# Delta rule: the first head's stages from the turning of the inverse on, two positions later

## The reference, cut to what matters

```python
a_mat = where(strict, einsum('bhnid,bhnjd->bhnij', k_beta, k) * decay, 0.0)
t_inv = triangular_solve(a_mat + eye, eye, lower=True, unit_diagonal=True)
u = einsum('bhnij,bhnjd->bhnid', t_inv, v * beta)
w = einsum('bhnij,bhnjd->bhnid', t_inv, k_beta * exp(g))
...
v_new = u_n - w_n @ state                 # step over the chunks
out   = q_n @ state + intra_n @ v_new
state = state * d_n + k_n.T @ v_new
```

## Time and profile before

| | |
|---|---|
| time, median of 3 runs | 1989.81 us (1989.42 to 1990.35) |
| the profiled execution's own time | 1988.39 us |
| its span, first to last instruction | 1986.6 us |
| PE busy | 1957.0 us (99%), 12159 instructions |
| DVE busy | 1385.5 us (70%) |
| ACT busy | 978.1 us (49%) |
| POOL busy | 518.5 us (26%) |
| mean granted TensorE clock | 0.998 |

### The profile page before, as it was taken

One profiled execution on the slowest core, in us unless ns is written; L12 is line 12 of the kernel. 1 busy time (PEld: TensorE's weight loads), 2 busy tenths in 40 slices (PEclk: granted clock), 3 DMA queues, 4 the chain that ended last, 5 costly groups with the idle time before them and its releaser, 6 DMA issues.

```text
span 1986.6 us, 30677 instructions
## 1 busy us (share of the span) xinstructions
PE 1957.0 (99%) x12159; PEld 1730.5 (87%) x12159; DVE 1385.5 (70%) x1928; ACT 978.1 (49%) x1472; POOL 518.5 (26%) x530
## 2 busy tenths in 40 slices
PE   9999999999999999999999999999999999999998
PEld 7898998787788998998898999878888888989996
DVE  6964977588747955973894696376776558946963
ACT  5543653445645633653562464355564555524642
POOL 1201311454221301311130221157566011301311
PEclk9999999999999999999999999999999999999999
DMA  5232332444122232332233223223222122332331
GB/s 190 99 124 86 107 131 72 124 134 130 54 85 96 107 119 84 110 127 82 94 116 109 85 107 127 77 71 97 75 71 93 55 95 96 115 109 85 117 128 43
DMA packets 63168, 199.97 MB, mean 101 GB/s; under 512 B 12816, under 2 KB 14896, under 8 KB 63024
## 3 DMA queue, kind: packets, MB, share of 16 engines
q1 hardware_dynamic: 59616, 196.55, 29.1%
q10 hardware_dynamic: 3408, 1.44, 0.3%
HBM read 188.51 MB, written 2.38 MB: 96 GB/s over the span
## 4 chain that ended last, share of the span: by engine, by line
PE 87%; DVE 6%; ACT 3%; issue 2%; POOL 1%; DMA 1%; SPq 0%; ACTq 0%; DVEq 0%; POOLq 0%
PE prod L592 16%; PE prod L594 15%; PE prod L593 15%; PE misc L686 6%; PE misc L688 6%; PE misc L687 6%; PE prod L686 4%; PE prod L688 4%; PE prod L687 4%; PE misc L907 2%; DVE h_lo L1621 1%; ACT L1445 0%; ACT h_hi L1158 0%; PE misc L786 0%; PE prod L752 0%
## 5 line engine op out<-in xcount | busy, mean ns | idle before, releaser
L592 PE MATMUL prod<-h_hi,p_hi 128*128 128x512 f32 x728 | 300.3, 413 | 2.2 <-DVE p_lo L1505 1.3
L594 PE MATMUL prod<-h_hi,p_lo 128*128 128x512 f32 x728 | 284.9, 391 | 0.0
L593 PE MATMUL prod<-h_lo,p_hi 128*128 128x512 f32 x728 | 284.0, 390 | 0.0
L592 PE MATMUL prod<-a_hi,d_hi 128*128 128x512 f32 x693 | 270.0, 390 | 0.0
L593 PE MATMUL prod<-a_lo,d_hi 128*128 128x512 f32 x693 | 270.0, 390 | 0.0
L594 PE MATMUL prod<-a_hi,d_lo 128*128 128x512 f32 x693 | 269.9, 389 | 0.0
L2102 POOL TENSOR_TENSOR s_f<-raw 128x512 f32<-128x512 f32 x70 | 94.4, 1348 | 670.0 <-DVE s_lo L1580 360.0
L1505 DVE TENSOR_TENSOR d_lo<-raw,d_hi 128x1408 fp32r<-128x1408 f32 x64 | 104.0, 1626 | 232.5 <-ACT d_hi L1072 232.5
L1072 ACT ACTIVATE d_hi<-raw 128x1408 fp32r<-128x1408 f32 x64 | 88.3, 1380 | 219.4 <-PE prod L594 218.9
L1505 DVE TENSOR_TENSOR p_lo<-raw,p_hi 128x1024 fp32r<-128x1024 f32 x86 | 111.9, 1301 | 75.5 <-ACT p_hi L1072 75.3
L592 PEld LDWEIGHTS prod<-h_hi,p_hi 128*128 128x128 f32 x728 | 137.1, 188 | 30.8 <-issue 8.5
(11 more groups left out here) (371 smaller groups left out, 5266.4 us busy)
## 6 DMA issues: line engine op xcount, KB each, us to landing
raw<-in_w SPq DMA_DIRECT2D x252, 512.0 KB, 3.5
raw<-in_wd SPq DMA_DIRECT2D x64, 704.0 KB, 4.1
blk<-blocks SPq DMA_DIRECT2D x16, 256.0 KB
x<-in_x SPq DMA_DIRECT2D x8, 256.0 KB, 5.7
k_dup<-k_dup SPq DMA_DIRECT2D x8, 256.0 KB, 3.5
silu_g<-g_rows SPq DMA_DIRECT2D x7, 256.0 KB, 4.6
out<-y_out SPq DMA_DIRECT2D x12, 128.0 KB, 2.0
raw<-in_w SPq DMA_DIRECT2D x4, 256.0 KB, 5.5
```

The source lines that it names most:

```text
L592: pe.matmul(bank, wh, hi, start=k == 0, stop=False)
L593: pe.matmul(bank, wh, lo, start=False, stop=False)
L594: ins = pe.matmul(bank, wl, hi, start=False, stop=k == tiles_n - 1)
```

## The change

In the first head alone, the seven stages `turn`, `y5`, `t5`, `y6`, `t6`, `y7` and `t7` get positions of their own. Until now they followed from `CHAIN1`: 36 plus 12, 14, 16, 18, 20, 22 and 24, so 48, 50, 52, 54, 56, 58 and 60. They come to stand at 50, 52, 54, 56, 58, 60 and 61. The first six are moved by two positions, the last by one. `new0` stays at 62. All four engines take their part of a stage from this table, so the parts on PE, ACT and DVE are moved alike; POOL and SP have no part in these seven stages.

```diff
 SLOT_0 = {"spread": 10, "decay": 14, "mask": 15, "tri": 16, "kk": 14, "amat": 17, "blocks": 18, "lvl5": 19, "qdec": 22, "lvl6": 20,
-          "lvl7": 25, "rows": 24}
+          "lvl7": 25, "rows": 24, "turn": 50, "y5": 52, "t5": 54, "y6": 56, "t6": 58, "y7": 60, "t7": 61}
```

## The result

| | before | after |
|---|---|---|
| median of 18 runs each, in the same rounds | 1990.67 us (1988.61 to 1996.86) | 1994.49 us (1992.22 to 1997.05) |
| ratio | | 1.0014, 95% interval 1.0008 to 1.0020 |
| span of the profiled execution | 1986.6 us | 1991.5 us |
| mean granted clock | 0.998 | 0.996 |

The change makes the kernel 0.14% slower, 2.8 us (1.6 to 4.0): small, but clear of 1. The two medians as such lie further apart, 3.8 us; the ratio with its interval is what is used here. Applied to the 1989.81 us from which the forecast started the ratio gives 1992.6, 0.9 above the forecast of 1991.7. The median as such, 1994.49, lies half a microsecond above the range; the median of the kernel before is itself 0.9 higher over its 18 runs than over the first three of them, from which the forecast started.

What follows compares the result with a forecast made beforehand. PE was taken to bound the kernel, 87% of the chain of waits. Waits of 0.9 us plus clock 1.0 made 1.9 us slower than 1989.81, so 1991.7 us; range 1988.8 to 1994.0, its own range 1990.3 to 1993.0.

Steps and rivals of the forecast that it cites:

- PE at `turn`: At the first head's transposes, PE's wait for GpSimd's `t_inv` shrinks from 2.38 to 1.02 us, a gain of 1.36.
- ScalarE's copy behind the stores and the tap: ScalarE's `u_inv` copy falls behind the second head's block stores and tap `vc`, starting at 1336.32 instead of 1331.92.
- PE at `y5`: PE reaches `y5` at 1333.11 as before and now waits 3.91 us for ScalarE's copy, until 1337.02.
- The rest of the chain: Behind `y5` on PE: no wait at `t5` and `y6`, at most 0.1 us together at `t7` and `new0`.
- the tight end: `y7` to `t7` and `t7` to `new0`, each one product shorter, wait at most 0.1 us together.
- Sum of the waits: PE's waits in these stages go from 4.12 to 5.03 us, a loss of 0.9.
- GpSimd behind `y5`: The second head's row substitution uses up its idle time and begins 0.2 us later; its `turn` waits no more than before.
- The clock: PE's clock may fall to half behind the `y5` wait: 0 to 2.0 us more, middle 1.0 taken.
- The sign that hung on this term: If right, `new0` comes some 0.8 to 3 us later, counted from the product at 1328.62.
- the copy is not held: Rival: ScalarE reaches `u_inv` by 1332.5, `y5` doesn't wait; 3.1 us faster, 1986.7; chance 0.13.
- Nothing measurable: Rival: a later wait that doesn't follow PE takes up the delay; 1989.8 us; chance 0.09.
- Slower than forecast: Rival: clock low for the whole 2.0, GpSimd late for the second head's `turn`; 4.5 us slower, 1994.3; chance 0.12.

Runs made afterwards that it cites:

- The halves run alone: Changed kernel with ScalarE's part of `turn` at 48: 0.9996 of before; kernel before with ScalarE's part of `turn` alone at 50: 1.0017.
- the kernel with the wait filled: Changed kernel with 16 extra matmuls of constants on PE ahead of `y5`'s wait in the first head: 1.0004 of before.
- the second profile: The changed kernel, unaltered, run once more against the kernel before in the same rounds: 1.0014 of before.
- the second kernel spaced by engine: Changed kernel with PE's stages at 51 to 63, ScalarE's `turn` at 48 and `y6` at 55, DVE's `t5` at 52 and `t6` at 58: 0.9989 of before.
- the stores behind the copy: Changed kernel with ScalarE's three block stores of the second head at position 50, behind the first head's `turn` copy, instead of 49: 1.0006 of before.
- the spaced one: Changed kernel with `turn` 49, `y5` 51, `t5` 55, `y6` 58, `t6` 59, `y7` 60, `t7` 61: 0.9992 of before, twice.

## Why the prediction was right, step by step

GpSimd in order of time after, for the fourth point (the second head's level-6 mask, then its row substitution):

```profile
...
1346.44 1.29 POOL L2080 TENSOR_TENSOR b_lvl<-a_mat,consts 128x512 f32<-128x512 f32 x1 [3.62 <-PE misc L907]
...
1348.05 0.29 POOL L2183 TENSOR_TENSOR rows_tmp<-blk,rows 128x60 f32<-128x60 f32 x1
...
```

- *PE at `turn`*: a wait of 1.02 worked out, 1.11 measured.
- *ScalarE's copy behind the stores and the tap*: the copy was to start 2.53 after the first of the three issues (1336.32 - 1333.79) and did (1337.54 - 1335.01). The halves run alone show that this is the loss, and that the rest of the change adds nothing that can be measured.
- *PE at `y5`*: 3.91 worked out, 3.89 measured. *The rest of the chain*: no wait at `t5` and `y6`, about 0.1 at the tight end, as worked out. Sum of the waits: 5.03 forecast, 1.11 + 3.89 + 0.1 = 5.1 measured, so 1.0 more than before, where 0.9 was forecast.
- *GpSimd behind `y5`*: the row substitution of the second head began at 1348.05, with no idle time ahead of it. The cover was used up, but by far more than worked out: counted from `turn` the substitution began 2.8 us later than before (1348.05 - 1332.45 against 1344.01 - 1331.23), not 0.2, because PE read `y6`'s tile later at the low clock. The conclusion holds all the same: PE itself was 3.4 us late by then, and its waits after 1360 us show none for the second head's `t_inv`.
- *The clock* is the term that was mis-sized: 1.0 taken, between bounds of 0 and 2.0; 2.4 to 2.5 measured (3.4 less the 1.0 of the waits; the kernel with the wait filled gives 2.5), and 3.2 in the second profile (4.1 less 0.9). The upper bound assumed that the lower level lasts no longer than the wait. It lasted 6.8 us, and 5.2 of them held work (1338.2 to 1343.4): half of that is 2.6. The middle was no reading of the rows either: of two idles of about the same length one was followed by a fall and one was not, and the idle to come was longer than both. The sign that hung on this term failed: `new0` came 3.35 us later, counted from the second head's `kk` (26.21 against 22.86), outside the 0.8 to 3 that were named.
- *The sum*: 1.9 forecast, 2.8 (1.6 to 4.0) measured by the ratio, 3.4 and 4.1 in the two profiles. The mechanism and the waits were right; that a clock term of less than half the size still left the sum inside the interval is partly luck.
- *The rivals*: "the copy is not held" did not come about. The run with all but ScalarE's part of `turn` lets the copy be in time by other means; its timing lies 0.8 us below before (0.9996, not told from 1), not 3.1, because `t5` then waits for the next copy behind the same stores and the same tap. "Nothing measurable" falls with an interval above 1. "Slower than forecast" was nearer with its clock term, 2.0, but its late GpSimd shows in no wait of PE.

## What to carry to other kernels

A stage that several engines share has a place in each engine's queue, and moving it by its place in one moves it past other things in the others: look, on each engine, at what lies between the old place and the new, and at when that is released. Here PE gained 1.3 us at one wait and lost 3.9 at the next, because ScalarE's part slid behind three DMA issues and a tap, both of which wait for the second head's `a_mat`. And a wait on PE is priced with the clock behind it: two kernels with nearly the same waits, filled and not filled, lay 2.5 us apart in that stretch.

## What the hardware showed that was not expected

- *The clock and the length of an idle.* It fell 2.3 us into PE's wait in one profile of the changed kernel (1334.3 to 1336.6) and 3.9 us into the same wait in the other, and behind a wait of 1.2 us in the second kernel spaced by engine; it stayed at 1.00 through the 2.2 us ahead of `turn` in the kernel before and the 2.5 us there with ScalarE's part of `turn` alone. The length of a wait does not tell by itself whether the clock falls; what else does, the runs leave open. Once low it stayed so for 6.8 us in three profiles and 3.4 in two, with PE at work most of that time. The Trainium skill, "TensorE: Matmul & The Clock Gate", section "Part 1: The HAM clock gate", says that the clock falls when TensorE has idled and comes back only after a stretch of sustained work. The return agrees: at 1343.4 in the changed kernel, 5.2 us after PE was at work again. That idling decides the fall agrees only in part, with 1.2 us followed by one and 2.5 us not.
- *DMA issues on ScalarE* hold what stands behind them, and run beside an operation that stands ahead of them once that has been let go. In the changed kernel the tap waited for all three issues (1335.01 to 1336.87), though its input was there at 1335.57 (DVE's evacuation, 1334.89 plus 0.68). With the stores behind the copy, the issues began at 1337.16, beside the tap (1337.15) that they stand behind; their own input `a_mat` had been there since 1336.51 (1335.39 plus 1.12), so they did wait for the tap to be released.
- *The same point of the program* was reached up to 3.5 us apart in profiles of kernels that are alike up to there (`kk` at 1326.50 to 1329.99). Differences of some microseconds between spans say nothing alone; distances inside the trace, from a point ahead of the change to one behind it, held to 0.7 us for the changed kernel run twice, and to 0.03 us for the spaced one.
